# The down product of every sixth expert step split around the next gate and up product

## The reference, cut to what matters

```python
def expert_block(args):
    xb, e = args
    return (jax.nn.silu(xb @ w_gate[e]) * (xb @ w_up[e])) @ w_down[e]
```

## Time and profile before

| | us |
|---|---|
| median of 3 runs (lowest, highest) | 1343.91 (1342.39, 1345.8) |
| profiled execution, its own time | 1342.12 |
| span of the profiled execution | 1340.3 |
| TensorE busy | 1229.3 |
| VectorE busy | 441.0 |
| ScalarE busy | 178.0 |
| GpSimd busy | 69.0 |

### The profile page before, as it was taken

One profiled execution on the slowest core, in us unless ns is written; L12 is line 12 of the kernel. 1 busy time (PEld: TensorE's weight loads), 2 busy tenths in 40 slices (PEclk: granted clock), 3 DMA queues, 4 the chain that ended last, 5 costly groups with the idle time before them and its releaser, 6 DMA issues.

```text
span 1340.3 us, 13718 instructions
## 1 busy us (share of the span) xinstructions
PE 1229.3 (92%) x5050; PEld 512.6 (38%) x5050; DVE 441.0 (33%) x901; ACT 178.0 (13%) x375; POOL 69.0 (5%) x84
## 2 busy tenths in 40 slices
PE   6999989899999999898988989999999999988888
PEld 3445544545333333232322367453333333322322
DVE  4386646566112221222121135551222222112112
ACT  2302116622000000000000011220000000000000
POOL 0122000000000000000000000000000000000000
PEclk9999989999999999998999999999999999989999
DMA  9958667375999999999999992859999999999995
GB/s 354 393 217 338 246 254 304 121 291 215 397 423 422 422 421 422 422 421 422 422 422 422 415 408 110 339 212 401 422 421 422 421 421 422 422 422 422 422 421 227
DMA packets 81216, 486.54 MB, mean 363 GB/s; under 512 B 6176, under 2 KB 7712, under 8 KB 32032
## 3 DMA queue, kind: packets, MB, share of 16 engines
q1 hardware_dynamic: 79168, 481.91, 88.1%
q10 hardware_dynamic: 2016, 4.21, 0.9%
HBM read 485.04 MB, written 1.05 MB: 363 GB/s over the span
## 4 chain that ended last, share of the span: by engine, by line
PE 60%; SPq 17%; DMA 14%; DVE 4%; ACT 2%; issue 2%; DVEq 0%; ACTq 0%
PE PS L807 20%; SPq L307 13%; DMA ring<-in_moe_w_up 12%; PE PS L826 10%; PE PS L615 8%; PE PS L835 5%; SPq L312 4%; PE PS L939 2%; PE PS L958 2%; PE PS L688 2%; PE PS L585 2%; PE PS L799 2%; DMA ring<-in_attn_w_in 2%; PE PS L817 1%; PE PS L644 1%
## 5 line engine op out<-in xcount | busy, mean ns | idle before, releaser
L807 PE MATMUL PS<-ring,KQH 128*64 128x512 f32 x2048 | 482.1, 615 | 34.1 <-DMA ring<-in_moe_w_up 32.6
L807 PEld LDWEIGHTS PS<-ring,KQH 128*64 128x64 f32 x2048 | 146.5, 141 | 316.4 <-issue 278.3
L826 PE MATMUL PS<-ring,KQH 128*64 128x512 f32 x1024 | 230.8, 592 | 0.9 <-ACT KQH L1151 0.9
L826 PEld LDWEIGHTS PS<-ring,KQH 128*64 128x64 f32 x1024 | 73.0, 137 | 146.8 <-issue 145.4
L1680 DVE TENSOR_TENSOR TMP<-PS,TMP 64x512 f32<-64x512 f32 x64 | 44.1, 689 | 232.4 <-PE PS L826 231.4
L1680 DVE TENSOR_TENSOR TMP<-PS,KQH 64x512 f32<-64x512 f32 x64 | 44.1, 689 | 230.9 <-PE PS L826 229.9
L835 PE MATMUL PS<-TMP,KQH 128*128 128x512 f32 x256 | 118.4, 605 | 1.6 <-DVE TMP L1680 1.6
L615 PE MATMUL PS<-ring,KQH 128*128 128x512 f32 x256 | 116.6, 599 | 0.0
L1157 ACT ACTIVATE KQH<-PS 128x256 f32<-128x256 f32 x62 | 23.8, 383 | 671.5 <-PE PS L807 671.5
L1697 DVE TENSOR_TENSOR KQH<-KQH,PS 128x256 f32<-128x256 f32 x64 | 38.7, 605 | 158.2 <-ACT KQH L1157 158.2
L447 POOL COPY KQH<-KQH 128x512 f32 x62 | 38.0, 614 | 839.5 <-PE PS L807 769.5
(11 more groups left out here) (237 smaller groups left out, 791.2 us busy)
## 6 DMA issues: line engine op xcount, KB each, us to landing
ring<-in_moe_w_gate SPq DMA_DIRECT2D x128, 1024.0 KB, 26.0
ring<-in_moe_w_up SPq DMA_DIRECT2D x128, 1024.0 KB, 26.7
ring<-in_moe_w_down SPq DMA_DIRECT2D x64, 2048.0 KB, 28.1
ring<-in_ada_w SPq DMA_DIRECT2D x23, 2048.0 KB, 16.2
ring<-in_attn_w_in SPq DMA_DIRECT2D x2, 4096.0 KB, 12.7
ring<-in_attn_w_in SPq DMA_DIRECT2D x2, 2048.0 KB, 20.8
ring<-in_attn_w_out SPq DMA_DIRECT2D x1, 4096.0 KB, 15.1
ring<-in_pool_w_in SPq DMA_DIRECT2D x1, 4096.0 KB, 24.8
```

The costliest lines, as they stand in the source:

```text
L807: ins = mm(PS[64 * f:64 * f + 64, 4, :], xs[:, k, 0:SLOTS], gu_w[s][:, :, k, 256 * f:256 * f + 256], start=k == 0, stop=k == KC - 1)
L826: ins = mm(PS[64 * f:64 * f + 64, 6, :], lhs, dn_w[s][:, c, 512 * f:512 * f + 512], start=c == 0, stop=c == 3)
```

## The change

The step with `c == BODY` makes the slices 0 and 1 of its down product, then the second part of the next expert's gate and up product, with its wait for the weights, then the slices 2 and 3 of the down product, with `dn_done` behind them. All other steps, and all other engines, are as before. No instruction is added or removed.

```diff
-            def down(s):
-                for c in range(4):
+            def down(s, cs=range(4)):
+                for c in cs:
                     a, b = divmod(c, 2)
                     lhs = t_sb[:, 256 + P * b + 64 * a:256 + P * b + 64 * a + 64]
...
-                    down(L.slot(c)).then_inc(L.dn_done, 1)
-                    if not last:
+                    if last:
+                        down(L.slot(c)).then_inc(L.dn_done, 1)
+                    elif c == BODY:
+                        down(L.slot(c), range(2))
+                        pe.wait_ge(L.gu2_in[L.slot(n)], (2 * it + n // 3) * 32 + 32)
+                        gate_up(L.slot(n), xw[n % 2], range(4, KC)).then_inc(L.gu_done, 1)
+                        down(L.slot(c), range(2, 4)).then_inc(L.dn_done, 1)
+                    else:
+                        down(L.slot(c)).then_inc(L.dn_done, 1)
                         pe.wait_ge(L.gu2_in[L.slot(n)], (2 * it + n // 3) * 32 + 32)
                         gate_up(L.slot(n), xw[n % 2], range(4, KC)).then_inc(L.gu_done, 1)
                     if c % 2:
```

## The result

| | kernel before | after the change |
|---|---|---|
| median of 11 runs, us | 1342.48 | 1346.07 |
| lowest to highest | 1341.34 to 1345.8 | 1342.69 to 1351.03 |
| profiled execution, own time | 1342.12 | 1344.75 |
| its span | 1340.3 | 1342.9 |

The ratio is 1.0029, with a 95% interval of 1.0015 to 1.0042: some 3.6 us slower by the medians (3.9 by the ratio) where 2.0 were forecast. The absolute time comes closer than that, 1346.07 for a forecast 1345.9, and this is luck: the forecast stood on a median of three runs, 1343.91, which eleven runs put 1.4 us lower, and that error nearly cancels the cost that was forecast too small. The runs of the changed kernel are also wider apart, 8.3 us against 4.5.

What follows compares the result with a forecast made beforehand. Transfers were taken to bound the experts' middle, a dependent chain each layer's end; ten steps lose 1.00 us, but only both steps 30 count: 1343.91 + 2.0 = 1345.9 us, range 1342.6 to 1349.3.

Steps and rivals of the forecast that it cites:

- TensorE's own work at 0: In all ten split steps the same 48 matmul records only run in another order, costing 0.
- +1.00 us behind the split step: Before the next transpose, VectorE's scalings now precede the hidden-value product: 2.10 us of idle against 1.10, +1.00 us.
- Eight middle steps at 0: Steps 6, 12, 18, 24 of both layers: each 1.00 us lost goes into later waits for weights, cost 0.
- the 3.0 us of the prediction: Lead that TensorE loses in sum over steps 6, 12 and 18, before the first waits for weights.
- SP's queue at 0: Down-weight loads issued 3.46 us later; step 6, the tightest, has some 10.0 us of transfers ahead, so cost 0.
- The sum, +2.0: Step 30 of both layers pays 1.00 us each: +2.0 us, median 1345.9 us, chance 0.55.
- The chain behind the router's load was taken to move along unchanged: After layer 0, the router's load and what follows start later by layer 0's +1.00 us, with no further cost.
- couldn't be told from no change: A slowdown of 0.15%, under the 0.3% (4.0 us) bound, was called the same; chance of the same 0.81.
- The rival of a fall in the tails: TensorE's clock falls behind step 30's longer idle, 1.7 us each: one fall chance 0.20, two 0.05.
- its two in seven: Of seven places with 2.0 to 2.7 us idle in the trace before, two had a clock fall.
- The closed gap: Rival: half a down product covers silu and product, each layer's tail gains 1.10 us, 1341.7 us; chance 0.05.

Runs made afterwards that it cites:

- Run 8: Kernel before, nothing split; in step 30 VectorE repeats its two scalings into unused memory between silu and the product: 1347.82 us, ratio 1.0051.
- run 5: Against the kernel before: step 30 alone split, VectorE makes hidden values ahead of its scalings there, its down product in bank 7: 1339.11 us, ratio 0.9979.
- run 6: Changed kernel with the split in all 15 even steps of each layer: 1350.36 us, ratio 1.007 to the kernel before.
- run 11: The changed kernel once more, unaltered: 1346.16 us, ratio 1.0028 to the kernel before.
- run 2: Changed kernel with the split in step 30 of each layer alone: 1347.56 us, ratio 1.0046 to the kernel before.
- run 4: Changed kernel plus two idle products of ones behind each split down product: 1343.63 us, ratio 1.002 to the kernel before.
- run 9: Kernel before with eight instead of five idle products ahead of the wait for the router's load between the layers: 1339.93 us, ratio 0.9979.
- run 10: Changed kernel with idle products behind each split down product and eight ahead of the router's wait: 1342.56 us, ratio 1.0001 to the kernel before.
- run 7: Split in step 30 alone, plus two idle products of ones in the longer gap: 1345.38 us, ratio 1.0034 to the kernel before.
- run 1: Changed kernel with the split in steps 6, 12, 18 and 24 alone, not in step 30: 1342.11 us, ratio 1.0001 to the kernel before.
- run 3: Changed kernel, VectorE making the hidden values ahead of the down product wait and scalings: 1342.04 us, ratio 1.0006 to the kernel before.

## Why the prediction was right, and where its size was off

- **TensorE's own work at 0.** Right: 1.72, 3.43 and 1.74 us in the chain for 1.72, 3.46 and 1.72.
- **+1.00 us behind the split step.** Right: 1.01 us in the tail, 1.02 in the table of waits for each of ten. Run 8 shows it without the split; run 5 takes it away with the split in place.
- **Eight middle steps at 0.** Right for these: 1.0001 with them alone. TensorE's lead shrank by more than the 3.0 us of the prediction, though: the clock fell behind step 6 in both layers and behind step 12 of layer 1 (5.20, 5.35 and 5.35 us for 3.65), at 1.6 to 1.7 us each. The waits for weights took that up too.
- **SP's queue at 0.** Right for step 6 and later. In the changed kernel step 6's release went out at 985.36, which is 3.4 us later counted from the layer's first down product, and landed after 14.0 us for 17.5: it still had 6.5 us of other transfers ahead. The argument (transfers ahead of the delayed one against its delay) also tells where it ends: in step 2 only 1.9 us were ahead for a delay of 3.4, and run 6 pays some 2 us per layer.
- **The sum, +2.0.** The direction and the range held, the size came out larger: 3.6 us here and 3.8 in run 11, though both intervals begin at or under 2.0. The term that best fills the difference is TensorE's clock, which I had looked for in one of two places. In the tails it does fall at times (run 2, both tails; run 6, one; the change's two traces, none), and run 4 with that gap filled was nearer to 2.0. The other place is what follows layer 0. The chain behind the router's load was taken to move along unchanged, but it grew by 1.64 us in the traces. Runs 9 and 10 show that the clock between the layers is worth time; they don't separate 2.0 from 3.8 us for the change itself. That the loss couldn't be told from no change held for three runs only: with eleven and twelve, both intervals lie above 1.
- **The rival of a fall in the tails.** It was priced right (5.37 us for 3.68 in run 2) and its two in seven is near the three of eight seen since. The rule that the prediction took from the page "TensorE: Matmul & The Clock Gate" of the Trainium skill, section "HAM oscillation — how this bites in real kernels", was stretched: the waits in the page's example are of some 3 to 5 us, and the tail's are of 2.1 and 0.5.
- **How the 1.64 us hangs together with the change is not shown.** The stretch took 9.7 us in all seven traces in which step 31's transposes of layer 0 were made to wait longer or, with idle products in the gap, came as late (the change twice, runs 2, 4, 6, 7, 8), and 8.1 us in all four without (before, runs 1, 3, 5). It doesn't go with how far the execution as a whole had come: the router's first product came at 779.99 us in run 7 and at 780.44 in run 11, both earlier than the 782.52 of the kernel before. What does tell the two groups apart is where the half clock sets in. In the seven it set in between 0.2 us before the first router product and 0.9 us behind it, and lasted about twice as long as in the four, where it set in 1.4 to 2.1 us behind it. Why transposes that are 1 us late should go with an early onset remains open, since the wait before the product is 2.7 to 2.9 us in both groups. If they had nothing to do with each other, so clean a division of eleven traces would come up once in 330 times; but the pattern was found in these traces, and only run 11 was made to test it.
- **The closed gap.** Rightly held unlikely: silu was early and nothing came of it until VectorE's order was turned (run 3), and only bank 7 (run 5) made it a gain.

## What to carry to other kernels

When work is moved behind another piece, look at the engine that consumes it: a queue written by hand may wait for the moved piece first, and hold back what the critical engine needs next. In a kernel bound by its transfers, price such a loss by place: free where transfers stand in line, paid in full in the last step and wherever the line is empty, as at a layer's start. And when a wait is removed, follow the waiting engine's queue one instruction further, down to the bank it writes, before the gain is booked.

## What the runs showed of the hardware

- The same 16 + 4 + 16 matmul records between the layers took 8.1 or 9.7 us, with the half clock for a shorter or a longer part of them, and 6.43 us with the 2.7 us wait ahead of them filled by three more products of ones, which nobody reads. So this wait for a load of 128 KB costs 1.7 or 3.3 us in clock behind it, besides itself. The Trainium skill, page "TensorE: Matmul & The Clock Gate", section "HAM oscillation — how this bites in real kernels", has it that a wait between bursts of matmuls throttles the burst behind it, with waits of some 3 to 5 us in its example. The traces agree, and have it for waits of 2.7 to 2.9 us in all eleven with this wait unfilled; they add that the same wait can cost either amount.
- The down product of step 31 takes 3.68 us at full clock and 5.37 us behind 2.14 + 0.46 us of idle when the clock has fallen. It fell in three of eight tails with this gap unfilled (the change twice, runs 2 and 6), and in neither of run 8's two, where the gap was 2.52 us.
